# Routed experts of a fused transformer kernel: down projection in three split passes instead of one fp32 product, and the gated rows turned ahead of the next gate/up product

## The reference, cut to what matters

```python
def swiglu(t, w_gu, w_dn):
    g, u = jnp.split(t @ w_gu, 2, axis=-1)
    return (jax.nn.silu(g) * u) @ w_dn

def one_block(args):
    rb, e = args
    return swiglu(t_pad[rb], w_gu[e], w_dn[e]).astype(jnp.float32)
```

## Time and profile before

| | |
|---|---|
| three runs | 3028.26, 3028.45, 3032.71 us; median 3028.45 us |
| profiled execution | 3033.24 us, of which the span of the records is 3031.4 us |
| mean granted clock of TensorE | 0.988 of full speed |
| TensorE busy | 2919.9 us, 96% of the span |
| VectorE busy | 1646.6 us, 54% |
| ScalarE busy | 1186.9 us, 39% |
| DMA, mean over the span | 183 GB/s |
| part of the span with the blocks of experts | from about 477 to 1144 us |

### The profile page before, as it was taken

How to read it: one execution, slowest core, us unless ns; L and a number is a source line. 1 busy time by engine, 2 the same in 40 slices (tenths; PEclk the granted TensorE clock), 3 DMA queues, 4 the chain that set the end, 5 groups by cost and what they waited for, 6 DMA issues and landing times. The chain is left out here.

```text
span 3031.4 us, 38143 instructions
## 1 busy us (share of the span) xinstructions
PE 2919.9 (96%) x13588; PEld 2265.1 (75%) x13588; DVE 1646.6 (54%) x1973; ACT 1186.9 (39%) x1378; POOL 267.7 (9%) x425
## 2 busy tenths in 40 slices
PE   6999799999999999999999999999999999999998
PEld 4886566767767667888877788887888877788886
DVE  7746857666666657555256555524554246543322
ACT  4124634666666653323136432213232135432312
POOL 0100002222222230000000000000000000000000
PEclk9989999999999999999999999999999999999999
DMA  7543237999999987554222255422554222132221
GB/s 295 182 160 116 80 135 266 360 357 360 370 352 346 359 335 274 201 194 152 97 95 76 70 208 194 166 97 97 197 192 164 91 94 84 56 107 94 95 94 68
DMA packets 115474, 555.49 MB, mean 183 GB/s; under 512 B 20544, under 2 KB 22080, under 8 KB 73152
## 3 DMA queue, kind: packets, MB, share of 16 engines
q1 hardware_dynamic: 88896, 491.43, 44.4%
q0 software_dynamic: 26496, 62.96, 5.9%
HBM read 549.10 MB, written 37.75 MB: 194 GB/s over the span
## 5 line engine op out<-in xcount | busy, mean ns | idle before, releaser
L168 ACT ACTIVATE stream_high<-stream_raw 128x2048 fp32r<-128x2048 f32 x151 | 289.3, 1916 | 799.5 <-PE ffn_ps_psum L560 754.8
L173 DVE TENSOR_TENSOR stream_low<-stream_raw,stream_high 128x2048 fp32r<-128x2048 f32 x156 | 356.8, 2287 | 406.6 <-ACT stream_high L168 406.2
L558 PE MATMUL ffn_ps_psum<-h_high_f,stream_high 128*128 128x512 f32 x1344 | 523.2, 389 | 0.0
L560 PE MATMUL ffn_ps_psum<-h_high_f,stream_low 128*128 128x512 f32 x1344 | 522.8, 389 | 0.0
L559 PE MATMUL ffn_ps_psum<-h_low_f,stream_high 128*128 128x512 f32 x1344 | 522.8, 389 | 0.0
L311 DVE TENSOR_TENSOR expert_low<-expert_raw,expert_high 128x2048 fp32r<-128x2048 f32 x128 | 293.4, 2292 | 217.5 <-ACT expert_high L307 215.3
L559 PEld LDWEIGHTS ffn_ps_psum<-h_low_f,stream_high 128*128 128x128 f32 x1344 | 252.3, 188 | 52.9 <-issue 0.2
L558 PEld LDWEIGHTS ffn_ps_psum<-h_high_f,stream_high 128*128 128x128 f32 x1344 | 252.3, 188 | 52.4 <-issue 0.2
L560 PEld LDWEIGHTS ffn_ps_psum<-h_high_f,stream_low 128*128 128x128 f32 x1344 | 252.3, 188 | 52.1
L307 ACT ACTIVATE expert_high<-expert_raw 128x2048 fp32r<-128x2048 f32 x128 | 244.2, 1909 | 114.2 <-PE experts_g_psum L560 114.2
L558 PE MATMUL ffn_ps_psum<-ffn_hid_high,stream_high 128*128 (+1 forms) x704 | 277.6, 394 | 3.2 <-DVE ffn_sg L782 3.2
(11 more groups left out here) (486 smaller groups left out, 4527.6 us busy)
## 6 DMA issues: line engine op xcount, KB each, us to landing
expert_raw<-in_exp_gu SPq DMA_DIRECT2D x128, 1024.0 KB, 9.3
stream_raw<-in_ffn_gu SPq DMA_DIRECT2D x88, 1024.0 KB, 4.9
expert_raw<-in_exp_dn SPq DMA_DIRECT2D x64, 1024.0 KB
con<-in_w_mod SPq DMA_DIRECT2D x120, 512.0 KB
stream_raw<-in_ffn_dn SPq DMA_DIRECT2D x44, 1024.0 KB, 4.9
mix_mod_rows<-in_w_ada POOLq DMA_DIRECT2D x32, 512.0 KB, 4.9
stream_raw<-in_w_in SPq DMA_DIRECT2D x16, 1024.0 KB, 5.0
pieces_raw<-in_w_in SPq DMA_DIRECT2D x13, 1024.0 KB, 6.2
```

What stands on the lines that cost most here:

```text
L168: self.nc.scalar.activation(self.high[:, q], self.raw[:, q], ACT.Copy).then_inc(self.high_done, 1)
L173: self.nc.vector.tensor_tensor(self.low[:, q], self.raw[:, q], self.high[:, q].bitcast(F32), ALU.subtract)\
L558: mm(out, w[0], x[0], start=start, stop=False)
L560: return mm(out, w[1], x[0], start=False, stop=stop)
```

## The change

The down weights of a block are cut by ScalarE into `dn_high` (two pieces of 128x1024) and by VectorE into `dn_low`; the turned gated rows are cut by ScalarE into `ht[:, 0]` and by VectorE into `ht[:, 1]`. `down` becomes 12 fp32r passes. The parts have one slot each, so their writers wait for the down product of the block before (`y_done`). From round 1 on `turn_h(n)` stands ahead of `gate_up(n+1)` on TensorE. The raw down slot is released when its low parts are made. `hidden` now writes into `sg`, which takes the memory of `rstd`; `dn_high` takes that of the first half of the shared expert's weights, whose columns are laid out as four contiguous parts. The function `mm3` is unchanged.

```diff
@@ -285,6 +285,7 @@
         self.raw, self.high, self.low = tiles
+        self.d_high, self.d_low = k.sem("d_high"), [k.sem(f"d_low{j}") for j in range(2)]
         self.up_in = [[k.sem(f"up{j}_loaded{s}") for j in range(2)] for s in range(2)]
@@ -311,11 +312,27 @@

+    def down_piece(self, s, j):
+        return self.raw[:, s, 2, j * D:(j + 1) * D]
+
+    def split_down_high(self, nc, act, r, s):
+        act.wait_ge(self.down_in[s], 16 * (r + 1))
+        act.wait_ge(self.y_done, 2 * r + s)
+        for j in range(2):
+            nc.scalar.activation(self.dn_high[:, j, :], self.down_piece(s, j), ACT.Copy).then_inc(self.d_high, 1)
+
+    def split_down_low(self, engine, eng, r, s, j):
+        eng.wait_ge(self.d_high, 4 * r + 2 * s + j + 1)
+        eng.wait_ge(self.y_done, 2 * r + s)
+        engine.tensor_tensor(self.dn_low[:, j, :], self.down_piece(s, j), self.dn_high[:, j, :].bitcast(F32), ALU.subtract)\
+            .then_inc(self.d_low[j], 1)
+
     def wait_up(self, sp, r, s):
...
     def wait_down(self, sp, r, s):
-        sp.wait_ge(self.y_done, 2 * r + s - 1)
+        for j in range(2):
+            sp.wait_ge(self.d_low[j], 2 * r + s - 1)

@@ -2157,9 +2174,13 @@
             even = tile("even_rows", [P, TOPK, D])
-            hid, hT, wg = tile("shared_hid", [P, 2, S]), tile("hT", [P, KD, S]), tile("shared_wg", [P, KD, 2 * EH])
+            hid, hT = tile("shared_hid", [P, 2, S]), tile("hT", [P, KD, S])
+            with nc.sbuf_tensor("expert_dn_high", [P, 2, D], F32R) as dn_high:
+                pass
+            wg = tile("shared_wg", [P, 4, KD, P])
             with self.stage("weights"):
                 weights, tables = ExpertWeights(self, expert_tiles), Tables(self)
+                weights.dn_high = dn_high
                 block_expert, used_pairs = self.sb("block_expert", [1, P], I32), self.sb("used_pairs", [1, 1], I32)
@@ -2224,7 +2245,7 @@
                         for k in ks:
-                            m = mm(ps[:, FOUR + i, :], wg[:, k, i * P:(i + 1) * P], hT[:, k, :], start=k == 0, stop=k == KD - 1)
+                            m = mm(ps[:, FOUR + i, :], wg[:, (0, 2, 1, 3)[i], k, :], hT[:, k, :], start=k == 0, stop=k == KD - 1)
                         if ks[-1] == KD - 1:
@@ -2411,7 +2432,9 @@
             idx, out_idx = ([self.sb(f"{name}{s}", [P, 1], U32) for s in range(2)] for name in ("idx", "out_idx"))
-            sg, hx, ht, y = self.sb("sg", [P, 2, EH]), self.sb("hx", [P, 2, EH]), self.sb("ht", [P, 2, EH]), self.sb("y", [P, 2, D])
+            sg = self.rstd[:].rearrange("p (s n) -> p s n", s=2)
+            ht, hsum, y = self.sb("ht", [P, 2, EH], F32R), self.sb("sums", [P, EH]), self.sb("y", [P, 2, D])
+            weights.dn_low = self.sb("dn_low", [P, 2, D], F32R)

@@ -2420,20 +2443,20 @@
             stored = [self.sem(f"stored{s}") for s in range(2)]
-            (idx_ready, out_idx_ready, x_turned, x_high, x_low, gu_done, silu_done, hid_done, h_turned, h_copied,
+            (idx_ready, out_idx_ready, x_turned, x_high, x_low, gu_done, silu_done, hid_done, h_turned, h_high, h_low,
              y_high, y_free, idx_seen, y_seen, experts_out, back, chain_s, late_found) = self.sems(
-                "idx_ready out_idx_ready x_turned x_high x_low gu_done silu_done hid_done h_turned h_copied y_high y_free idx_seen y_seen experts_out back chain late_found")
+                "idx_ready out_idx_ready x_turned x_high x_low gu_done silu_done hid_done h_turned h_high h_low y_high y_free idx_seen y_seen experts_out back chain late_found")
             w_low, y_done = weights.w_low, weights.y_done
...
             wd = xg
-            red = ht[:, 0, :].rearrange("p (c t) -> p c t", c=2)
+            red = hsum[:].rearrange("p (c t) -> p c t", c=2)
             sq = hT
...
             down_place = lambda s: raw[:, s, 2].rearrange("p (c n) -> p c n", c=2)
-            wg_place = wg[:].rearrange("p k n -> p (k n)").rearrange("p (c n) -> p c n", c=TT)
+            wg_place = wg[:].rearrange("p i k n -> p (i k n)").rearrange("p (c n) -> p c n", c=TT)

@@ -2458,7 +2481,7 @@

-            def pipelined(eng, steps, late_steps=None, start=0, between=None):
+            def pipelined(eng, steps, late_steps=None, start=0, between=None, after=None):

@@ -2473,7 +2496,7 @@
                                 step(r, q)
-                                if s == 1 and between:
+                                if s == 1 and between and step is after:
                                     between()
@@ -2642,19 +2665,20 @@
                         for k in range(2):
-                            mm = nc.tensor.transpose(psH[:, 0, k * P:(k + 1) * P], hx[:, s, k * P:(k + 1) * P], ident)
+                            mm = nc.tensor.transpose(psH[:, 0, k * P:(k + 1) * P], sg[:, s, k * P:(k + 1) * P], ident)
                         mm.then_inc(h_turned, 1)
...
                         n = 2 * r + s
-                        pe.wait_ge(weights.down_in[s], 16 * (r + 1))
-                        pe.wait_ge(h_copied, n + 1)
+                        pe.wait_ge(h_low, n + 1)
                         pe.wait_ge(y_high, n + 1)
-                        wd = raw[:, s, 2].rearrange("p (k n) -> p k n", k=2)
-                        for half in range(2):
-                            for k in range(2):
-                                mm = nc.tensor.matmul(psY[:, half, :], ht[:, s, k * P:(k + 1) * P], wd[:, k, half * S:(half + 1) * S],
-                                                      start=k == 0, stop=k == 1)
+                        for k in range(2):
+                            pe.wait_ge(weights.d_low[k], n + 1)
+                            c = slice(k * P, (k + 1) * P)
+                            for half in range(2):
+                                o = slice(half * S, (half + 1) * S)
+                                mm = self.mm3(psY[:, half, :], (ht[:, 0, c], ht[:, 1, c]), (weights.dn_high[:, k, o], weights.dn_low[:, k, o]),
+                                              start=k == 0, stop=k == 1)
                         mm.then_inc(y_done, 1)
@@ -2680,16 +2704,16 @@
                         table(2 + s, 1)
-                    steps = [(1, gate_up), (0, turn_h), (2, turn_x), (0, down)]
+                    steps = [(0, turn_h), (1, gate_up), (2, turn_x), (0, down)]
                     mm = nc.tensor.matmul

-                    def shared_up(b, i):
+                    def shared_up(b):
                         for k in range(KD):
-                            m = mm(psX[:, b, :], wg[:, k, i * P:(i + 1) * P], hT[:, k, :], start=k == 0, stop=k == KD - 1)
+                            m = mm(psX[:, b, :], wg[:, 2 + b, k, :], hT[:, k, :], start=k == 0, stop=k == KD - 1)
                         m.then_inc(up_done, 1)

-                    pipelined(pe, steps + [(AHEAD, table)], steps + [(AHEAD, late_table)], start=1, between=lambda: shared_up(0, 1))
-                    shared_up(1, 3)
+                    pipelined(pe, steps + [(AHEAD, table)], steps + [(AHEAD, late_table)], start=1, between=lambda: shared_up(0), after=turn_h)
+                    shared_up(1)

@@ -2753,7 +2777,8 @@
                         act.wait_ge(h_turned, 2 * r + s + 1)
-                        nc.scalar.activation(ht[:, s, :], psH[:, 0, 0:EH], ACT.Copy).then_inc(h_copied, 1)
+                        act.wait_ge(y_done, 2 * r + s)
+                        nc.scalar.activation(ht[:, 0, :], psH[:, 0, 0:EH], ACT.Copy).then_inc(h_high, 1)

@@ -2775,8 +2800,19 @@
                         a(hid[:, 1, :], psX[:, 0, :], ACT.Silu).then_inc(up_silu, 1)
-                    pipelined(act, [(2, lambda r, s: split(r, s, 0)), (1, silu), (0, copy_h), (2, copy_x),
-                                    (2, lambda r, s: split(r, s, 1)), (0, copy_y)], between=shared_silu)
+
+                    def split_down(r, s):
+                        weights.split_down_high(nc, act, r, s)
+                    for s in range(2):
+                        split_down(0, s)
+                        split(1, s, 0)
+                        silu((s + 1) // 2, (s + 1) % 2)
+                        copy_h(0, s)
+                        copy_x(1, s)
+                        split(1, s, 1)
+                        copy_y(0, s)
+                    pipelined(act, [(0, split_down), (0, copy_h), (2, lambda r, s: split(r, s, 0)), (1, silu), (2, copy_x),
+                                    (2, lambda r, s: split(r, s, 1)), (0, copy_y)], start=1, between=shared_silu, after=copy_h)
                     nc.scalar.preload_act_table_set(LOG_EXP)
@@ -2847,7 +2883,15 @@
                         dve.wait_ge(silu_done, 2 * r + s + 1)
-                        nc.vector.tensor_tensor(hx[:, s, :], sg[:, s, :], psG[:, s, EH:2 * EH], ALU.mult).then_inc(hid_done, 1)
+                        nc.vector.tensor_tensor(sg[:, s, :], sg[:, s, :], psG[:, s, EH:2 * EH], ALU.mult).then_inc(hid_done, 1)
+
+                    def low_h(r, s):
+                        dve.wait_ge(h_high, 2 * r + s + 1)
```

(13 more changed lines are left out.)

## The result

The changed kernel takes **3094.5 us** (median of 4 runs, 3059.4 to 3111.2), the kernel before 3028.7 beside it (3028.3 to 3032.7): a ratio of **1.018** between the means, 95% interval 1.009 to 1.026; the ratio leaves out the longest run, which counts as a slow one. The forecast was 3014; the time lies in the direction, and beyond the size, of the rival "the scatter chain lengthens". The runs differ by 52 us where those of before differ by 4; the profiled execution is the shortest, 3059.37 us, and its span of 3057.5 us is 26.1 over the 3031.4 of before. All that follows on it is read against that, and the loss of a median run is larger.

A forecast was written before the change was run, and what follows sets the result against it. TensorE's instructions were taken to bound the experts at 10.244 us a block, DMA close behind. Blocks -21.5, last two -1.4, start +3.3 and scatters +5 gave -14.6: 3018.6 profiled, 3014 us median, range 2998 to 3036.

The forecast's parts named there:

- the scatter chain lengthens: Rival at GpSimd's wait for landings: busier DMA engines lengthen landings, at 9.2 us 3044 us; chance 0.15 with other slower ends.
- Item 1: TensorE's down product as three split passes: 3.44 to 2.75 us, TensorE's sum 9.57 us a block.
- Items 2 and 3: New down pieces: ScalarE 0.95 us each, VectorE 1.14 each, beside TensorE's work unless they come too late.
- Item 4: Waits among ScalarE, VectorE and TensorE for the new instructions: 19.77 us for two blocks, 9.885 us a block.
- the ring: Circle of handovers from ScalarE to VectorE to TensorE, said to set 9.885 us a block, steps alternating 9.57 and 10.20.
- Item 5: Weight loads: 9.73 or 8.9 us a block, under 9.885, cost none; a quoted skill rule would give 10.2.
- Item 6: GpSimd's scatters, one landing before the next: 10.1 us a block, longer than 9.885, costing +5 us.
- The reserve: Time a needed scatter landing is seen before ScalarE's copy_y: 7.7 us, to be used up at 0.2 us a block.
- Item 7: First two blocks, written by hand: VectorE comes late, down(0) waits until 497.7 instead of 492.78; cost +3.3 us.
- TensorE alone: Rival: TensorE's 9.57 us a block decides, 2990 us, about 3002 half way; chance 0.14 for nearer to this.
- the transfers: Rival: DMA transfers bound the experts at 10.2 us a block, 3028 us; chance 0.18, including a sum of small losses.
- the change did what it said: Opposite of a rival: pieces might not overlap, 1.22 on VectorE and 1.02 on ScalarE apiece, +9 us, 3023.

The follow-up runs named there:

- e3: The changed kernel with only block 0's down weights split, later blocks multiplying by those parts: 3039.3 us, ratio 1.002 to the kernel before.
- e4: The changed kernel with the gated rows turned behind the next gate/up, as before the change: 3140.5 us, ratio 1.037 to the kernel before.
- e6: The changed kernel with two scatters in flight and ScalarE's copy_h ahead of its two down pieces: 3019.9 us, ratio 0.996 to the kernel before.
- e10: The changed kernel with two scatters in flight, copy_h ahead of the down pieces, and low_h(0) ahead of VectorE's split at the start: 3017.1 us, ratio 0.995.
- e2: The changed kernel with GpSimd making a scatter's row numbers before waiting for the last landing, one scatter in flight: 3036.4 us, ratio 1.001.
- e1: The changed kernel with two scatters allowed in flight instead of one: 3024.5 us, ratio 0.997 to the kernel before.
- e11: The changed kernel with the gathers from block 6 on replaced by a 1 KB copy, one scatter in flight: 3021.0 us, ratio 0.998.

## Why the prediction was wrong, point by point

- **Item 1, the down product**: right. Passes 0.23 us apart, 2.88 us from the first pass of down to the next product on TensorE (646.60 to 649.48).
- **Items 2 and 3, the pieces**: right within 0.05. ScalarE's pair takes 1.89 us (640.62 to 642.51) for 1.90, VectorE's 2.26 for 2.28.
- **Item 4, the ring**: right in kind, short by 0.12 us a block. Predicted were 9.57 and 10.20 in turn, 9.885 on average; measured 9.7 to 9.8 and 10.2 to 10.3, 10.00. e3, without the pieces, has 9.6. The waits of gate_up for the low x are 0.39 us on average (13.3 in 34), where some 0.64 was forecast. The missing term is at copy_y. The ring let it start 0.20 us behind the end of down, but it stands behind ScalarE's own split. From the changed kernel's timelines of TensorE and ScalarE:

```profile
645.81 1.03 PE L2651 MATMUL experts_x_psum<-con,weights_xg 128*128 128x128 f32 x8
646.60 0.48 PE L575 MATMUL experts_y_psum<-expert_dn_high,experts_ht 128*128 128x512 f32 x1
```

```profile
646.88 1.03 ACT L2785 ACTIVATE experts_xh<-experts_x_psum 128x1024 fp32r<-128x1024 f32 x1 [0.49 <-PE experts_x_psum L2651]
647.80 1.90 ACT L308 ACTIVATE expert_high<-expert_raw 128x2048 fp32r<-128x2048 f32 x1
649.79 1.11 ACT L2791 ACTIVATE experts_y<-experts_y_psum,weights_table 128x1024 f32<-128x1024 f32 x1
```

  From the start of down (646.60) to the copy are 0.28 + 0.92 + 1.99 = 3.19 us, where the ring had 2.75 + 0.20 = 2.95: 0.24 for two blocks. That turning the gated rows early gives cover was right too, and e4 shows what the old order costs.
- **Item 5, the loads**: right for the changed kernel. ScalarE has no notable wait for weights, and the rate reaches 373 GB/s at a share of 0.97 inside the experts, so the bound that item 5 quotes did not hold here. The 3.65 MB a block are what the records hold, and too few: by the shapes of the tiles a block moves 3.15 MB of weights and twice 0.52 MB of rows, 4.19 MB, and from 600 to 700 us the software queue's records have 4.87 MB where ten blocks of rows have 10.5. The GB/s in this document are too low for that reason. In other kernels the loads do show: ScalarE waits for weights for 21 to 23 us in e6 and e10, and for 49 in e2.
- **Item 6, the scatters: the step that failed.** It set +5, from a chain of 10.1 us: the landing of before (8.7, seen after 0.25), the CAST at 0.18, preparation 0.96. It had the place and the waiter right, and by e3 nearly the size for a lighter loop. But it added the chain to the loop as fixed numbers, and they are not fixed. In the bound turns the CAST takes 1.04 us, since it falls into VectorE's low split, and the landing is seen after 9.44 instead of 8.95: 11.48 us a turn, 1.4 over the forecast, of which the CAST has 0.86 and the landing 0.49. That lasted for 31 blocks of the profile, +34.9 us; more blocks in the slow rhythm would explain the longer runs, which have no trace. The reserve failed too: it was to go at 0.2 us a block, and most of it was gone by block 7. The rival had named this mechanism with a landing of 9.2 us and 3044. With 0.25 until it is seen that is what the bound turns have on average (9.44), but the rival had no term for the CAST, and its chance of 0.15 rested on an argument that failed: that longer blocks relieve the DMA engines. The share does fall, to 0.85, and landings get longer all the same.
- **Item 7, the start**: the wait of down(0) was forecast as 497.7 - 492.78 = 4.9 us and is 4.86. The cost was not 3.3 but 7.4. Of the 4.1 more, 2.4 are twelve passes at 0.43 instead of 0.23, for which the sum had no term; 0.7 lie in the first gate/up product, which takes 6.8 us and took 6.2 before, since its passes came to 0.23 later. The gate/up passes behind down(0) are 0.23 apart again from 498.97 on and cost nothing more. The last 1.0 is not traced.
- **Taken together**: with the chain away (e1) the change gives 8 us (3024.5 against 3032.6 on that chip). The forecast of -14.6 had +5 in it for scatters: without them -19.6, less 60 x 0.12 = 7 for the ring and 4 for the start, is -8.6. The rest of the sum fits, and the scatters decided the sign. That it fits to 1 us is in part luck: the interval of e1 reaches from -13 to -2 us.
- **The other rivals**: TensorE alone did not decide (e3's first blocks show its 9.6, e6 comes nearest); the transfers bound nothing directly in the changed kernel, but by way of the landing they are part of the cause; the change did what it said.

**Still open.** A turn of the chain has two parts that grew, and taking away either is enough: e2 takes the CAST out of it, e11 shortens the landing, and both lose the slow rhythm. The CAST is traced: with the reserve gone, ScalarE's copy starts when the landing is seen, and VectorE's low split has begun shortly before (899.99 and 900.61 above), so the CAST meets it, in 22 turns of 29. Why landings are longer in the slow rhythm, at a smaller share, is not shown. The loads' issue stands in a fixed distance to the scatter there, and they may meet it each time; that is an argument only. Untested is the direct cure for the CAST: VectorE's low splits moved away from it, or the row numbers made by another engine.

## What to carry to other kernels

A chain with one transfer in flight has a period of its own (landing, seen, prepared, issued), and it must be compared with the loop that the change makes, not with the one it finds; when it comes within a few tenths of a microsecond, give it a second transfer in flight before making the loop faster. Neither part of it is a constant: the landing depends on what the DMA engines do beside it, and the preparation on what another engine does at that moment, so look at which instructions will run beside it once something waits for the chain. And of a stall on TensorE count the passes behind it as well.

## What the runs showed of the hardware

- A scatter of 128 rows of 4 KB lands 8.2 us after issue (median) in windows of 336 GB/s without other row traffic, 8.3 to 8.8 with the gathers in the kernel before, in e3 and in the good stretch of the changed kernel, 9.2 to 10.0 in the bad stretches; 512 KB a block on the hardware queue does what the gather on the software queue does.
- The same kernel runs in two rhythms, 10.0 and 11.4 us a block, and changes between them within one execution; a median over runs then hides a mixture.
- GpSimd's CAST of 128 numbers takes 0.18 us in the earlier trace rows. One that starts while VectorE is in an instruction of 2.29 us with two operands in SBUF lasts until that ends, up to 2.3 us (48 of 49 in the changed kernel); beside an instruction with an operand in PSUM it takes 0.18 to 0.20. No line of the waits shows it, since the CAST itself is longer.
- TensorE's passes were 0.43 us apart behind a wait of 4.86 us, and from the third pass behind one of 1.85 us in e4's stage, where such a wait comes in each block; behind a single wait of 2.33 us they stayed at 0.24.
